# Output projections of a streaming encoder walked third by third, with the next norm cut into parts inside them

## The reference

```python
for li in range(DEPTH):                       # DEPTH = 2
    hp = rmsnorm(yp, attn_norm[li]); hs = rmsnorm(ys, attn_norm[li])
    if li % 2 == 0: mp, ... = mixer_ab(hp, ...); ms, ... = mixer_ab(hs, ...)
    else:           mp, sp_ = mixer_c(hp, ...);  ms, ss_ = mixer_c(hs, ...)
    yp = yp + mp; ys = ys + ms                # mixer's last step: (mixed values) @ w_out
    yp = yp + swiglu(rmsnorm(yp, ffn_norm[li]), ffn_w_in[li], ffn_w_out[li])
    ys = ys + swiglu(rmsnorm(ys, ffn_norm[li]), ffn_w_in[li], ffn_w_out[li])
y_prompt, y_sample = rmsnorm(yp, final_norm), rmsnorm(ys, final_norm)

def rmsnorm(x, g):
    return x * lax.rsqrt(jnp.mean(x * x, axis=-1, keepdims=True) + EPS) * g
def swiglu(h, w_in, w_out):
    a, b = jnp.split(h @ w_in, 2, axis=-1)
    return (jax.nn.silu(a) * b) @ w_out       # hidden width 2816
```

## Time and profile before

| | us |
|---|---|
| median of three runs | 3308.49 (3307.04 to 3311.26) |
| the profiled execution, its own time | 3303.76 |
| its span, first to last instruction | 3302.0 |
| PE busy | 3081.4 (93% of the span) |
| DVE busy | 1459.8 (44%) |
| ACT busy | 726.5 (22%) |
| POOL busy | 97.0 (3%) |
| mean granted TensorE clock | 0.956 of full |

### The profile page before, as it was taken

The page is one execution under the profiler, slowest core; times in us unless marked ns, Lnnn a source line. Parts: engine busy times, 40 slices in busy tenths (PEclk is TensorE's granted clock), DMA queues, the critical chain, the costliest instruction groups (busy, mean ns, idle before and its releaser), DMA issues.

```text
span 3302.0 us, 45486 instructions
## 1 busy us (share of the span) xinstructions
PE 3081.4 (93%) x18140; PEld 2963.6 (90%) x18140; DVE 1459.8 (44%) x2480; ACT 726.5 (22%) x1160; POOL 97.0 (3%) x88
## 2 busy tenths in 40 slices
PE   6997699979999999999899999996979999999997
PEld 5996366879999999999799999995979999999996
DVE  6887534242333333334454545545253333333335
ACT  3111556222111111111311112111031111111111
POOL 3000000010000000000100000000010000000001
PEclk9999769989999999999999999996989999999998
DMA  3112500201111111111211111110201111111111
GB/s 122 45 45 60 209 1 1 96 19 52 52 39 45 39 39 43 40 44 34 83 40 40 40 40 40 41 39 10 113 26 45 40 44 39 45 40 44 46 38 58
DMA packets 47750, 163.13 MB, mean 49 GB/s; under 512 B 8416, under 2 KB 15888, under 8 KB 44768
## 3 DMA queue, kind: packets, MB, share of 16 engines
q1 hardware_dynamic: 42992, 148.45, 13.1%
q10 hardware_dynamic: 3456, 8.91, 0.8%
q0 software_dynamic: 1136, 3.27, 0.5%
HBM read 143.28 MB, written 18.92 MB: 49 GB/s over the span
## 4 chain that ended last, share of the span: by engine, by line
PE 87%; DVE 6%; issue 3%; ACT 3%; POOL 1%; DMA 1%; DVEq 0%; ACTq 0%; POOLq 0%; SPq 0%
PE PS L493 19%; PE PS L495 19%; PE PS L494 19%; PE PS L735 5%; PE PS L737 5%; PE PS L736 5%; PE PS L1376 4%; PE PS L1112 2%; PE PS L1141 2%; DVE HF L604 1%; PE PS L1121 1%; POOL SQ L405 1%; DVE HBL L614 1%; PE PS L1392 1%; DVE Y L959 1%
## 5 line engine op out<-in xcount | busy, mean ns | idle before, releaser
L493 PE MATMUL PS<-HAH,WH 128*128 128x384 f32 x1872 | 648.2, 346 | 21.1 <-DVE HBL L1720 5.8
L494 PE MATMUL PS<-HAL,WH 128*128 128x384 f32 x1872 | 633.1, 338 | 0.0
L495 PE MATMUL PS<-HAH,WL 128*128 128x384 f32 x1872 | 632.2, 338 | 0.0
L493 PE MATMUL PS<-HBH,WH 128*128 128x384 f32 x1872 | 625.8, 334 | 0.0
L495 PE MATMUL PS<-HBH,WL 128*128 128x384 f32 x1872 | 625.6, 334 | 0.0
L494 PE MATMUL PS<-HBL,WH 128*128 128x384 f32 x1872 | 625.5, 334 | 0.0
L481 DVE TENSOR_TENSOR WL<-WR,WH 128x1024 fp32r<-128x1024 f32 x200 | 243.2, 1224 | 561.5 <-ACT WH L476 560.0
L493 PEld LDWEIGHTS PS<-HAH,WH 128*128 128x128 f32 x1872 | 357.6, 191 | 30.9 <-issue 22.9
L735 PE MATMUL PS<-UH,WH 128*128 128x384 f32 x1056 | 360.9, 342 | 5.2 <-issue 5.0
L494 PEld LDWEIGHTS PS<-HAL,WH 128*128 128x128 f32 x1872 | 357.7, 191 | 2.8 <-issue 2.1
L737 PE MATMUL PS<-UH,WL 128*128 128x384 f32 x1056 | 359.7, 341 | 0.0
(11 more groups left out here) (196 smaller groups left out, 2663.1 us busy)
## 6 DMA issues: line engine op xcount, KB each, us to landing
WR<-w_fi_in SPq DMA_DIRECT2D x88, 512.0 KB, 3.7
WR<-w_fo_in SPq DMA_DIRECT2D x44, 512.0 KB, 3.7
WR<-w_c_in SPq DMA_DIRECT2D x32, 512.0 KB, 4.1
WR<-w_ab_in SPq DMA_DIRECT2D x20, 512.0 KB, 3.8
CACHES<-k_cache_in SPq DMA_DIRECT2D x8, 1024.0 KB, 7.5
CACHES<-v_cache_in SPq DMA_DIRECT2D x8, 1024.0 KB, 6.1
X<-x_t_in SPq DMA_DIRECT2D x3, 1536.0 KB, 11.0
x_spill<-X SPq DMA_DIRECT2D x1, 4608.0 KB, 12.3
```

Of the source, the lines that this page charges most:

```text
L493: nc.tensor.matmul(out, wh, hh(k, third(n)), start=(k == 0), stop=False)
L494: nc.tensor.matmul(out, wh, hl(k, third(n)), start=False, stop=False)
L495: mm = nc.tensor.matmul(out, wl, hh(k, third(n)), start=False, stop=(k == KT - 1))
```

## The change

Both output projections now walk third by third: for third n all eight output blocks, then the next third. The products go to banks 3 to 7 in turn, and each of the 24 steps has its own weight block, so every block is loaded and cut three times. The residual comes back in four DMAs (third 0 in two parts, then thirds 1 and 2); in layer 1 each third's DMA waits only for that third's cut. While third n is multiplied, the norm of third n-1 is worked off in parts, one part per step, on ACT and DVE; POOL folds no more here. The last third's norm lies under the first four products of the swiglu, whose gate and other block now alternate by third. The loops of the projection are written out.

```diff
+        def reload(sp, src, free=None):
+            for i, (n, ks) in enumerate(((0, slice(0, 2)), (0, slice(2, KT)), (1, slice(0, KT)), (2, slice(0, KT)))):
+                if free:
+                    free(n)
+                sp.dma_start(X[:, ks, third(n)], src[:, ks, third(n)]).then_inc(s_xr[i], 16)
...
         def proj_sp(sp, T, w):
-            with sp.Fori(0, KT // 2 - 1) as i:
...
+            for p in range(2, N3 * KT):
+                weights(sp, T, p % 2, w[p % KT, :, :])
...
-            sp.wait_ge(s_hlo, H_CO)
...
+            reload(sp, xd.rearrange("p (k t) -> p k t", k=KT), lambda n: sp.wait_ge(s_hlo, H_C + 2 * (n + 1)))
...
+        def proj_pe(pe, T, ready, late=None):
+            for p in range(N3 * KT):
+                n, m = divmod(p, KT)
+                have(pe, T, p % 2)
+                if m == 0:
+                    ready(n)
+                need(pe, s_x, T("x") - 4)
+                if p in (3, 4) and late:
+                    late(p + 3)
+                T.add("x")
+                product(PS[:, 3 + p % 5, 0:TH], p % 2, n).then_inc(s_xo, 1)
+                if n and m == 0:
+                    rms_sums(pe, T, n - 1)
+                if n and m == 1:
+                    rms_cast(pe, T, n - 1)
...
+        def proj_act(act, T, stored=None):
+            for p in range(N3 * KT):
+                n, m = divmod(p, KT)
+                cut_hi(act, T, 1 - p % 2, None if p == 0 else (s_xo, T("x")))
...
+                if n and m == 0:
+                    part_squares(act, T, n - 1, 2)
+                if n and m == 1:
+                    part_root(act, T, n - 1)
+                if n and m == 3:
+                    part_hi(act, T, n - 1, 0)
+                if n and m == 4:
+                    part_hi(act, T, n - 1, 1)
+                if m == 4:
+                    part_squares(act, T, n, 0)
+                if m == 6:
+                    part_squares(act, T, n, 1)
...
+        def proj_dve(dve, T, reloaded, gain):
+            for p in range(N3 * KT):
+                n, m = divmod(p, KT)
+                cut_lo(dve, T, 1 - p % 2)
+                if n and m == 0:
+                    part_fold(dve, T, 2)
+                if n and m == 1:
+                    rms_diag(dve, T, n - 1)
+                if n and m == 2:
+                    rms_scale(dve, T, n - 1, gain, False, range(0, AB))
+                if n and m == 3:
+                    rms_scale(dve, T, n - 1, gain, False, range(AB, KT))
+                if n and m == 4:
+                    rms_lo(dve, T, n - 1, (0,))
+                if n and m == 5:
+                    rms_lo(dve, T, n - 1, (1,))
+                if m == 6:
+                    part_fold(dve, T, 0)
+                if m == 7:
+                    part_fold(dve, T, 1)
+                if p in (0, 2, KT, 2 * KT):
+                    dve.wait_ge(s_xr[(0, 2, KT, 2 * KT).index(p)], 16 * reloaded)
+                T.add("x")
+                need(dve, s_xo, T("x"))
...
+            def first_block():
+                have(pe, T, 0)
+                for n in range(N3):
+                    pe.wait_ge(s_hlo, base + 2 * (n + 1))
...
+                    product(PS[:, n, 0:TH], 0, n).then_inc(s_fa, 1)
+                    if n == 0:
+                        rms_sums(pe, T, 2)
+                        have(pe, T, 1)
+                        need(pe, s_x, T("x"))
...
+                    product(PS[:, 3 + n, 0:TH], 1, n).then_inc(s_fb, 1)
+                    if n == 0:
+                        rms_cast(pe, T, 2)
...
+            def last_norm():
+                part_squares(act, T, 2, 2)
+                cut_hi(act, T, 2, (s_xo, T("x")))
+                part_root(act, T, 2)
+                part_hi(act, T, 2, 0)
+                part_hi(act, T, 2, 1)
+                act.wait_ge(s_hlo, base)
```

More of the change, by code:

```diff
@@ L229, in encoder @@
         s_xo = sem("s_xo")
-        s_xr = [sem(f"s_xr{i}") for i in range(2)]
+        s_xr = [sem(f"s_xr{i}") for i in range(N3 + 1)]
         s_sp = sem("s_sp")
@@ L607, in rms_scale, with rms_lo @@
                     ins.then_inc(s_hf, 1)
-        def rms_lo(dve, T, n):
+        def rms_lo(dve, T, n, halves=(0, 1)):
             hf = HF1 if n % 2 else HF0
             for half, hi, lo in ((0, HAH, HAL), (1, HBH, HBL)):
+                if half not in halves:
+                    continue
                 T.add("hhi")
@@ L642, in link @@
             dve.wait_ge(s_dc, T("dc"))
[L645 to L697, removed]
@@ new lines, in encoder, with part_squares, part_root @@
+        SQ_PARTS = (slice(0, 4), slice(4, 6), slice(6, 8))
+        def part_squares(act, T, n, part):
+            act.wait_ge(s_x, T("x0") + n * KT + SQ_PARTS[part].stop)
+            if part == 0:
+                need(act, s_ms, T("ms"))
+                T.add("ms")
+            ks = SQ_PARTS[part]
+            act.activation(SQ[:, ks, :], X[:, ks, third(n)], ACT.Square).then_inc(s_sq, 1)
+        def part_root(act, T, n):
+            act.wait_ge(s_ms, T("ms"))
+            act.activation(rt[:, 3 * n:3 * n + 3], PS[:, n, TH:TH + TPT], ACT.Sqrt,
+                           bias=eps[:, 0:1], scale=1.0 / D).then_inc(s_rt, 1)
@@ new lines, in part_hi @@
+        def part_hi(act, T, n, half):
+            hf = HF1 if n % 2 else HF0
+            out = (HAH, HBH)[half]
+            T.add("hf")
+            act.wait_ge(s_hf, T("hf"))
+            act.activation(out[:, :, third(n)], hf[:, half * AB:(half + 1) * AB, :], ACT.Copy).then_inc(s_hhi, 1)
+        def proj_act(act, T, stored=None):
+            T.add("x0", T("x") - T("x0"))
+            for p in range(N3 * KT):
+                n, m = divmod(p, KT)
+                cut_hi(act, T, 1 - p % 2, None if p == 0 else (s_xo, T("x")))
+                T.add("x", 1)
+                if p == 4 and stored:
+                    stored()
+                if n and m == 0:
[10 more added lines that the diff above has]
+                    part_squares(act, T, n, 1)
@@ L818, in w_in @@
                     cut_lo(dve, T, 1 if j == 0 or first else 0)
-                    if j == 0:
+                    if j == 0 and first:
+                        last_norm()
+                    elif j == 0:
                         cut_lo(dve, T, 2)
```

99 lines of the change are left out of this document (57 added, 42 removed).

## The result

| | before | changed |
|---|---|---|
| median, us | 3309.88 (four runs, 3307.04 to 3313.70) | 3269.40 (four runs, 3259.82 to 3274.08) |
| ratio | 1 | 0.9873, 95% interval 0.9849 to 0.9898 |
| profiled execution, its own time | 3303.76 | 3274.08 |
| its span | 3302.0 | 3272.3 |

The kernel is 40 us faster; forecast were 40.0, and 3268.5 for the median (by the medians the gain is 40.5). Which 40 they are is read from the trace, engine by engine.

What follows compares the result with a forecast made beforehand. PE's work plus its gaps bound the kernel. Layer 0 wins 28.0 - 3.6 - 2.2 = 22.2 us, layer 1 27.4 - 1.3 - 6.1 - 2.2 = 17.8, together 40.0: 3268.5 us; own range 3262 to 3274, with rivals 3254 to 3281.

Steps and rivals of the forecast that it cites:

- What can go: Behind the output projections: norm and half clock cost 32.5 and 31.9 us; 28.0 (layer 0) and 27.4 (layer 1) can go.
- Last sum to third `UF`: From the projection's last sum to the swiglu's sixth product: 26.5 us, clock 1.00, no PE idle stretch above 1 us.
- Steps at no cost: Projection steps: cuts and norm parts on ACT and DVE fit within 4.165 us, cost 0; PE's norm matmuls stay, 4.5 per layer.
- reserve: Weight slots in the projection: 3.7 us of landing plus 2.4 of cuts make 6.1, against two products, 8.3 us.
- The last third's norm: Under the swiglu's first four products: ready at 17.7 to 18.3 us, fourth product ends at 18.1; no wait, bound 0.2 per layer.
- rival 2: Swiglu start: last third's norm 4 us late per layer, PE waits 8 us, twice 2.2 of clock; 3281 us, chance 0.16.
- The wait in layer 0: Projection start: third weight block behind the reload, PE waits 3.6 us (1.7 to 4.8), plus 2.2 of clock.
- rival 1: Projection starts: the reload is hidden anyway, only 1.3 us of wait remain, 54.1 won; 3254 us, chance 0.10.
- The waits in layer 1: Projection start: 1.3 us for slot 1's late low cut, 6.1 (4.1 to 9.6) for the third weight block, 2.2 of clock.
- The total: Both layers: 22.2 and 17.8 us won, together 40.0; profiled execution 3263.8, median 3268.5; chance 0.67.

Runs made afterwards that it cites:

- mended kernel: Changed kernel with third weight block ahead of the reload, later residual thirds in pieces between weights, layer 1's slot 1 cut earlier: median 3255.82 us, ratio 0.9836.
- experiment 4: Kernel before with only the new order, five banks and four reload DMAs, norm still behind the projection: median 3328.50 us, ratio 1.0062.
- Experiment 6: Changed kernel, but from the projection's fifth step each weight load waits until a further, unused 512 KB load has landed: 3306.80 us, timed once.
- experiment 5: Changed kernel with the swiglu's first six products back to gate, gate, gate, other, other, other: 3282.64 us, timed once.
- second execution: The changed kernel timed once more, nothing altered: median 3268.32 us, ratio 0.9884 to the kernel before.
- experiment 2: Changed kernel with the reload's four DMAs issued on GpSimd's queue, SP issuing only weights: 3258.87 us, timed once.

## Why the prediction was right

It was right in its total and in nearly all of its terms.

**What can go.** Forecast were 28.0 and 27.4 us. The mended kernel, which waits at neither start, shows it directly: 153.25 - 124.96 = 28.3 and 159.33 - 130.87 = 28.5; experiment 4 against the changed kernel, both with their waits at the starts, gives 27.2 and 29.7. Last sum to third `UF`: forecast 26.5, measured 26.63 and 26.27, at full clock.

**Steps at no cost.** Plain steps are 4.16 us apart. The norm's sums and cast add 0.60 and 0.65 to a step, where the prediction took 0.7 and 0.75: 3.75 a layer instead of 4.5, and in layer 1 most of the 1.1 us by which more could go than forecast. Experiment 6 shows that the weights had a reserve, as worked out, and that it is used up at 7.3 us of landing.

**The last third's norm.** Forecast ready 17.7 to 18.3 us behind the last sum, measured 17.3 (732.42 + 1.75 - 716.91). PE showed no idle time there, so rival 2 did not come true; experiment 5 shows the price that rival 2 gave for a late chain, its lateness and some 2 us of clock (7.79 and 2.0 in layer 0).

**The wait in layer 0.** Forecast 3.6 + 2.2 of clock, measured 3.09, and 6.1 together (131.05 - 124.96): the wait 0.5 too long, the clock 0.8 too cheap. The won time, 22.2, is as forecast, to the tenth by luck: 0.3 more was paid and 0.3 more could go. That rival 1 did not come true is the queue order: the third block went out 2.6 us behind the reload's first issue and landed 13.8 later.

**The waits in layer 1: the term that was too small.** Forecast 1.3 + 6.1 + 2.2 = 9.6, measured 1.48 + 7.46, and 11.9 together (142.72 - 130.87; 11.1 in the second execution). The first product of the third block came late because the weights had landed 17.2 us after PE's first product, not 15.5. The second parts of the first third (issued at 2291.04) and the last third (2297.30) landed like this:

```profile
X<-x_spill SPq DMA_DIRECT2D x1, 1152.0 KB, 6.2
...
X<-x_spill SPq DMA_DIRECT2D x1, 1536.0 KB, 9.4
```

The first third was in at 2297.2, 6.6 us behind its first issue instead of the 5.9 that the prediction took from an output DMA; the second one followed after 4.2 (7.5 behind its issue at 2293.96), about the 4.1 taken; the last one at 2306.7, 5.2 later instead of 4.1. The weights came 1.2 behind it, near the 1.4 taken. Why the last third took longer stays open. The rest of the miss is the clock, some 3.0 us instead of 2.2. Since 1.1 us more could go than forecast, 16.6 (17.4) were won instead of 17.8.

**The total.** 22.2 + 16.6 = 38.8 of the forecast 40.0. The first profiled execution is 10 us above the forecast on its own scale, since untouched code took longer in it: 3.9 us ahead of the first sum and 6.1 between 743 and 2291. The second one had a span of 3262.0, and the forecast's 3263.8 less the 1.8 outside it is the same; with single executions this far apart, that is luck too. The mechanism rests on the distances.

## What to carry to other kernels

Work that stands alone between two full stretches is worth hiding in parts under products that don't need it, and its price is what the regrouping asks for at the start: here 18 of 57 us went back, most of them because a block needed early stood behind a bulk transfer needed late. Put on a queue first what is needed first, and break the bulk into pieces that go between. When a chain is hidden under later work, count how many products stand above its end; two of them fewer cost here half of the gain.

## What the runs showed of the hardware that was not expected

- Pieces of 1.5 KB moved at 379 GB/s in the reload of layer 0, pieces of 9 to 28 KB at 446 to 448, in the same place and from the same tensor.
- Behind waits of PE of 1.49 and 1.60 us the clock stayed at 1.00; behind waits of 3.09 to 3.75 most of the next product ran at the lower level. Wait and clock together cost 6.1 us for a wait of 3.09, and 4.9 for one of 3.29 (experiment 4): there the wait ended at 618.77 and the clock was 1.00 from 622 on; in the changed kernel it ended at 619.63, and the clock was still 0.50 from 622 to 624 and 0.60 from 624 to 626.
- A block on another queue overtakes a bulk load: 512 KB landed 7.5 and 9.6 us behind their issue, ahead of a piece of 1.5 MB issued before them (experiment 2); behind the bulk on the same queue it took 13.8, alone 3.3.
- Code that no kernel here touches varies from execution to execution by more than some of the effects: the first sum of layer 0 stood between 608.1 and 615.1 us, and from the third `UF` of layer 0 to the first product of layer 1 it took 1538.6 to 1548.1. With it varies how long the clock stays at its lower level in the attention: from 480 to 500 us its mean was 0.79 in the mended kernel and 1.00 in the kernel before. Whether that is cause or only company, and the whole of it, wasn't tried. Gains of a few microseconds are therefore read here from the stretch itself.
